# Seven block products in place of eight in sixteen projection chunks of a two-layer fp32 encoder

## The reference, cut to what matters

```
xn = rms_norm(h, ln_mix[l])
proj = xn @ w_in          # layer 0: 256x1024 @ 1024x2500, layer 1: 256x1024 @ 1024x3072
... attention on the split columns of proj, then y @ w_out, h = h + ...
xn = rms_norm(h, ln_ffn[l]);  h = h + hier_moe(xn, ...)   # top-1 group, top-2 of its 8 experts, 32 experts in all
```

## Time and profile before

| what | value |
|---|---|
| three runs | 1186.55, 1188.04, 1189.02 us |
| the profiled execution, device time | 1187.87 us |
| its span | 1186.1 us |
| mean granted TensorE clock | 0.997 of 2.4 GHz |
| PE busy | 1122.9 us of the span |
| DVE, ACT, POOL busy | 217.2, 245.5, 115.7 us |
| HBM read | 441.49 MB, 373 GB/s over the span |

### The profile page before, as it was taken

The page is one execution under the profiler, slowest core; times in us unless marked ns, Lnnn a source line. Parts: engine busy times, 40 slices in busy tenths (PEclk is TensorE's granted clock), DMA queues, the critical chain, the costliest instruction groups (busy, mean ns, idle before and its releaser), DMA issues.

```text
span 1186.1 us, 14020 instructions
## 1 busy us (share of the span) xinstructions
PE 1122.9 (95%) x5006; PEld 503.1 (42%) x5006; DVE 217.2 (18%) x579; ACT 245.5 (21%) x572; POOL 115.7 (10%) x307
## 2 busy tenths in 40 slices
PE   8999999999999988889999999999999998888896
PEld 6876533333333332323487756333333333323232
DVE  2864431000000000000223234300000000000002
ACT  2144251111111111111112233411121111111111
POOL 0003021000110000000000000210011000000000
PEclk9999999999999999999999999999999999999999
DMA  6985589999999999999997354899999999999994
GB/s 242 333 362 228 201 318 429 429 425 429 427 428 428 429 428 429 427 428 428 422 365 309 107 214 184 336 428 426 428 428 427 428 427 430 428 429 427 427 429 203
DMA packets 48586, 443.28 MB, mean 374 GB/s; under 512 B 9564, under 2 KB 14744, under 8 KB 16792
## 3 DMA queue, kind: packets, MB, share of 16 engines
q1 hardware_dynamic: 47464, 441.34, 89.6%
q10 hardware_dynamic: 1072, 1.26, 0.3%
HBM read 441.49 MB, written 1.09 MB: 373 GB/s over the span
## 4 chain that ended last, share of the span: by engine, by line
PE 65%; DMA 31%; ACT 2%; DVE 1%; issue 1%; ACTq 0%; SPq 0%; POOL 0%; POOLq 0%; DVEq 0%
PE PS L1525 22%; DMA places<-in_moe_w_up 15%; PE PS L1534 12%; DMA places<-in_moe_w_gate 11%; PE PS L1277 9%; PE PS L1541 6%; PE PS L1409 5%; PE PS L1281 4%; DMA places<-in_moe_w_down 3%; PE PS L1289 1%; PE PS L1364 1%; DMA bias<-in_c_rel_bias 1%; PE PS L1393 1%; PE PS L1610 1%; PE PS L1494 1%
## 5 line engine op out<-in xcount | busy, mean ns | idle before, releaser
L1525 PE MATMUL PS<-places,mix 128*64 128x512 f32 x1984 | 442.7, 595 | 46.5 <-DMA places<-in_moe_w_up 30.9
L1525 PEld LDWEIGHTS PS<-places,mix 128*64 128x64 f32 x1984 | 140.9, 137 | 339.9 <-issue 276.0
L1534 PE MATMUL PS<-places,gain_att 128*64 128x512 f32 x960 | 213.8, 596 | 0.8 <-ACT gain_att L793 0.5
L1541 PE MATMUL PS<-mix 128*128 128x512 f32 x256 | 124.8, 608 | 0.0
L758 ACT ACTIVATE mix<-acts 128x512 f32 x120 | 76.3, 636 | 227.1 <-PE PS L1525 214.4
L1534 PEld LDWEIGHTS PS<-places,gain_att 128*64 128x64 f32 x960 | 65.9, 137 | 124.5 <-issue 122.7
L1277 PE MATMUL PS<-acts,places 128*128 128x256 f32 x448 | 103.2, 384 | 0.0
L1173 DVE TENSOR_TENSOR mix<-PS,mix 128x512 f32<-128x512 f32 x28 | 19.4, 692 | 418.0 <-PE PS L1525 418.0
L1277 PEld LDWEIGHTS PS<-acts,places 128*128 128x128 f32 x448 | 83.2, 190 | 14.9 <-issue 3.3
L526 POOL TENSOR_TENSOR sm<-sm 128x1 f32<-128x1 f32 x32 | 6.2, 193 | 692.4 <-PE PS L1616 659.5
L565 POOL TENSOR_SCALAR mix<-drop 128x64 f32<-128x64 f32 x128 | 72.2, 584 | 0.0
(11 more groups left out here) (223 smaller groups left out, 633.6 us busy)
## 6 DMA issues: line engine op xcount, KB each, us to landing
places<-in_moe_w_gate SPq DMA_DIRECT2D x56, 2048.0 KB, 24.9
places<-in_moe_w_down SPq DMA_DIRECT2D x54, 2048.0 KB, 32.4
places<-in_moe_w_up SPq DMA_DIRECT2D x52, 2048.0 KB, 30.2
places<-in_moe_w_gate SPq DMA_DIRECT2D x16, 1024.0 KB, 10.6
places<-in_moe_w_up SPq DMA_DIRECT2D x16, 1024.0 KB, 6.4
places<-in_moe_w_down SPq DMA_DIRECT2D x16, 1024.0 KB, 7.5
places<-in_c_w_in SPq DMA_DIRECT2D x12, 1024.0 KB, 20.4
places<-in_ab_w_in SPq DMA_DIRECT2D x8, 1024.0 KB, 14.2
```

The source lines that it names most:

```text
L1525: last = mm(PS[e * SLOTS:(e + 1) * SLOTS, 2 + part, :], xg[:, k, e * SLOTS:(e + 1) * SLOTS], w[e][:, kk, :], start=(k == 0), stop=(k == NK ...
L1534: last = mm(PS[e * SLOTS:(e + 1) * SLOTS, 6 + b, :], hidT[:, k, e * SLOTS:(e + 1) * SLOTS], w[e][:, 512 * b:512 * b + 512], start=(k == 0) ...
L1541: last = mm(PS[:, Y_BANK[q]], pickT[:, t], ye[:, 512 * b:512 * b + 512], start=first, stop=final)
```

## The change

A chunk's product is a 2x2 block product: the tokens in two halves by two halves of the contraction, the weights in two halves of the contraction by two halves of the 256 columns. Each block product is 4 matmuls of 128x128 held by 128 moving columns, and a plain chunk would need eight of them. With sums and differences of blocks made beforehand, seven are enough (Strassen's scheme, in Winograd's form). The change does this from position 4 on in layer 0 (six chunks) and from position 2 on in layer 1 (ten chunks). The four sums of the tokens are made once per layer by DVE; the four sums of the weights once per chunk by POOL, three of them in place, one in a tile that is free then; the seven products go to bank 6 (four) and bank 7 (three); DVE combines them in two visits in place of the one copy. All these chunks are DVE's now, none ACT's.

```diff
+WINO_FROM = (4, 2)
+def nth(layer, pos):
+    return pos - WINO_FROM[layer] + (len(ORDER[0]) - WINO_FROM[0] if layer else 0)
+def sums_before(layer):
+    return 4 if layer and WINO_FROM[0] < len(ORDER[0]) else 0
+def wino(layer, pos):
+    return pos >= WINO_FROM[layer]
 def events(layer):
...
         for quarter in range(4):
             out.append(("tile", pos, quarter))
+            if quarter == 1 and wino(layer, pos):
+                out.append(("sums", pos, None))
             if quarter == 3:
                 out.append(("copy", pos, None))
...
 def by_dve(layer, pos):
-    return ORDER[layer][pos] in BY_DVE[layer]
+    return wino(layer, pos) or ORDER[layer][pos] in BY_DVE[layer]
...
+        token_sum = acts[:, 0:NT * D].rearrange("p (s k n) -> p s k n", s=4, k=4)
+        partial = [at(5640, P), drop0[:, :]]
...
@@ gpsimd
+            def weight_sums(l):
+                for pos in range(WINO_FROM[l], len(ORDER[l])):
+                    n = nth(l, pos)
+                    b11, b12, b21, b22 = (weights_of(pos, i, j) for i in range(2) for j in range(2))
+                    pool.wait_ge(s_place[l][pos], 16)
+                    pool.tensor_tensor(first_sum(l, pos), two_by_two(b12), two_by_two(b11), ALU.subtract).then_inc(s_tsum, 1)
+                    pool.wait_ge(s_tsum, 4 * n + 1)
+                    pool.tensor_tensor(b12, b22, b12, ALU.subtract).then_inc(s_tsum, 1)
+                    pool.wait_ge(s_raw, 2 * n + 1)
+                    pool.wait_ge(s_tsum, 4 * n + 2)
+                    pool.tensor_tensor(b11, b12, b11, ALU.add).then_inc(s_tsum, 1)
+                    pool.wait_ge(s_raw, 2 * n + 2)
+                    pool.wait_ge(s_tsum, 4 * n + 3)
+                    pool.tensor_tensor(b21, b21, b11, ALU.subtract).then_inc(s_tsum, 1)
...
             for l in range(DEPTH):
+                weight_sums(l)
...
@@ vector
+            def token_sums(l):
+                a11, a12, a21, a22 = (tokens(i, j) for i in range(2) for j in range(2))
+                dve.wait_ge(s_xs, 2 * l + 2)
+                dve.tensor_tensor(token_sum[:, 0], a11, a21, ALU.subtract).then_inc(s_xsum, 1)
+                dve.tensor_tensor(token_sum[:, 2], a21, a22, ALU.add).then_inc(s_xsum, 1)
+                dve.wait_ge(s_xsum, sums_before(l) + 2)
+                dve.tensor_tensor(token_sum[:, 1], token_sum[:, 2], a11, ALU.subtract).then_inc(s_xsum, 1)
+                dve.wait_ge(s_xsum, sums_before(l) + 3)
+                dve.tensor_tensor(token_sum[:, 3], a12, token_sum[:, 1], ALU.subtract).then_inc(s_xsum, 1)
+            def four_read(l, pos):
+                n, c = nth(l, pos), quarters(l, pos)
+                p = PS[:, 6].rearrange("p (m n) -> p m n", n=P)
+                dve.wait_ge(s_four, n + 1)
+                if pos > WINO_FROM[l]:
+                    dve.wait_ge(s_pd[l], copies(l, pos - 1))
+                link(dve.tensor_copy(partial[l], p[:, 0]))
+                link(dve.tensor_tensor(c[:, 0], partial[l].unsqueeze(1).broadcast_to((P, 2, P)), p[:, 1:3], ALU.add))
+                dve.tensor_tensor(partial[l], c[:, 0, 1], p[:, 3], ALU.add).then_inc(s_read, 1)
+            def three_read(l, pos):
+                n, c = nth(l, pos), quarters(l, pos)
+                p = PS[:, 7].rearrange("p (m n) -> p m n", n=P)
+                dve.wait_ge(s_proj[l], pos + 1)
+                dve.wait_ge(s_read, n + 1)
+                link(dve.tensor_tensor(c[:, 0, 1], c[:, 0, 1], p[:, 1], ALU.add))
+                dve.tensor_tensor(c[:, 1], partial[l].unsqueeze(1).broadcast_to((P, 2, P)), p[:, 0:2], ALU.add)
+                dve.tensor_tensor(c[:, 0, 1], c[:, 0, 1], p[:, 2], ALU.add).then_inc(s_pd[l], 1)
             def mixer(l):
                 for what, n, _ in events(l):
-                    if what == "copy" and by_dve(l, n):
+                    if what == "copy" and wino(l, n):
+                        three_read(l, n)
+                    elif what == "copy" and by_dve(l, n):
...
                             lambdas()
+                            token_sums(0)
...
+                    elif what == "sums":
+                        four_read(l, n)
...                                                # layer 1, before its mixer
+                    dve.wait_ge(s_proj[l], 1)
+                    token_sums(l)
                 mixer(l)
@@ tensor
+            def seven_products(l, pos, quarter):
+                n, by_column = nth(l, pos), ORDER[l][pos] not in ((4, 5) if l == 0 else (8, 9, 10, 11))
+                def product(bank, m, a, b):
+                    for k in range(4):
+                        held, moved = (b[:, k], a[:, k]) if by_column else (a[:, k], b[:, k])
+                        last = mm(PS[:, bank, m * P:(m + 1) * P], held, moved, start=(k == 0), stop=(k == 3))
+                    return last
+                if quarter == 0:
+                    pe.wait_ge(s_place[l][pos], 16)
+                    if pos == WINO_FROM[l]:
+                        copied(l, ORDER[l][pos - 2])
+                    else:
+                        pe.wait_ge(s_read, n)
+                    product(6, 0, tokens(0, 0), weights_of(pos, 0, 0)).then_inc(s_raw, 1)
+                    product(6, 1, tokens(0, 1), weights_of(pos, 1, 0)).then_inc(s_raw, 1)
+                elif quarter == 1:
+                    pe.wait_ge(s_xsum, sums_before(l) + 3)
+                    pe.wait_ge(s_tsum, 4 * n + 2)
+                    product(6, 3, token_sum[:, 0], weights_of(pos, 0, 1))
+                    pe.wait_ge(s_tsum, 4 * n + 3)
+                    product(6, 2, token_sum[:, 1], weights_of(pos, 0, 0)).then_inc(s_four, 1)
+                elif quarter == 2:
+                    copied(l, ORDER[l][pos - 1])
+                    # first sum of the weights x token_sum 2: four matmuls into bank 7, part 1
...
+                    pe.wait_ge(s_xsum, sums_before(l) + 4)
+                    product(7, 2, token_sum[:, 3], weights_of(pos, 1, 1))
+                else:
+                    pe.wait_ge(s_tsum, 4 * n + 4)
+                    product(7, 0, tokens(1, 1), weights_of(pos, 1, 0)).then_inc(s_proj[l], 1)
```

More of the change, by code:

```diff
@@ L358, in build @@
         s_proj, s_pa, s_pd = per_layer("projected"), per_layer("proj_act"), per_layer("proj_dve")
+        s_xsum, s_tsum, s_raw = sem("token_sums"), sem("weight_sums"), sem("raw_products")
+        s_four, s_read = sem("four_products"), sem("four_read")
         s_is, s_ir, s_drop = sem("index_scores"), sem("index_relu"), sem("selection")
@@ L393, in proj_dst, with quarters, first_sum, tokens @@
             return qkC[:, 2 * c:2 * c + 2] if c < 8 else vC[:, :, (c - 8) * CW:(c - 7) * CW]
+        def quarters(l, pos):
+            c = ORDER[l][pos]
+            dst = proj_dst(l, c)
+            if c in (4, 5) if l == 0 else c >= 8:
+                return dst.rearrange("p i (j n) -> p i j n", n=P)
+            return dst.rearrange("p j (i n) -> p i j n", n=P)
+        def first_sum(l, pos):
+            if pos + 2 < len(ORDER[l]):
+                return quarters(l, pos + 2)
+            j = pos + 2 - len(ORDER[l])
+            if l:
+                return quarters(l, (2, 4)[j])
+            return (kqi[:, 1:3], bias[:, 13:16:2])[j].rearrange("p j (i n) -> p i j n", n=P)
+        def tokens(i, j):
+            return xT[:, 4 * j:4 * j + 4, i * P:(i + 1) * P]
+        token_sum = acts[:, 0:NT * D].rearrange("p (s k n) -> p s k n", s=4, k=4)
+        partial = [at(5640, P), drop0[:, :]]
+        def weights_of(pos, i, j):
+            return place(pos).rearrange("p (k n) -> p k n", n=CW)[:, 4 * i:4 * i + 4, j * P:(j + 1) * P]
         @block.sync
@@ L526, in carry_waits, with two_by_two @@
                 pool.tensor_tensor(spare[:, site:site + 1], half[:, 0:1], half[:, 0:1], ALU.mult)
+            def two_by_two(a):
+                return a.rearrange("p (a b) n -> p a b n", b=2)
+            def weight_sums(l):
[12 more added lines that the diff above has]
+                    pool.tensor_tensor(b21, b21, b11, ALU.subtract).then_inc(s_tsum, 1)
             pool.wait_ge(s_half, 1)
@@ L1246, in copied @@
                 pe.wait_ge((s_pd if by_dve(l, pos) else s_pa)[l], copies(l, pos))
+            def seven_products(l, pos, quarter):
[21 more added lines that the diff above has]
+                    copied(l, ORDER[l][pos - 1])
+                    t1 = first_sum(l, pos)
+                    for k in range(4):
+                        b = t1[:, k // 2, k % 2]
+                        held, moved = (b, token_sum[:, 2, k]) if by_column else (token_sum[:, 2, k], b)
+                        mm(PS[:, 7, P:2 * P], held, moved, start=(k == 0), stop=(k == 3))
+                    pe.wait_ge(s_xsum, sums_before(l) + 4)
[3 more added lines that the diff above has]
+                    product(7, 0, tokens(1, 1), weights_of(pos, 1, 0)).then_inc(s_proj[l], 1)
             def project_tile(l, pos, quarter):
+                if wino(l, pos):
+                    seven_products(l, pos, quarter)
+                    return
```

(1 more changed line is left out.)

## The result

The kernel after took 1194.26 us (median of four, 1192.35 to 1195.95) against 1187.3 us for the kernel before beside it (four runs, 1186.16 to 1189.02): the ratio is 1.0055 [1.0043, 1.0068]. It is slower by some 7 us. The forecast, 1187.3 us and most likely no change, was wrong, though the measured time lies in its range.

A forecast was written before the change was run, and what follows sets the result against it. PE was taken to bound the projections and DMA bytes the late experts, with mixer time passing through to the kernel. Mixer 0 at +5.05 and mixer 1 at -5.6 net -0.55 us: 1187.3 us, range 1182 to 1195.

The forecast's parts named there:

- DVE's reads: Both mixers: two DVE visits add 2.2 us a chunk; PE waiting for normalized rows booked at 0.3 us per mixer.
- POOL's sums: Each chunk: four 128x512 additions at 1.26 us, 5.3 us in all, hidden from PE by 0.15 us in eight chunks.
- rival 2: "POOL late": POOL's third sum makes PE wait, from 1.41 us an operation; at 2.1 us, 1194.8 us; chance 0.20.
- three signs of being wrong: PE waiting for POOL by more than 1 us, counts above 0.115 us, or the clock staying at 1.00.
- Rival 3: Mixer 0: each logit waits behind a DVE visit, 0.5 us at twelve steps, +5.7: 1193.0 us; chance 0.09.
- The matmuls: Seven-product chunks: 0.110 us a count, 6.16 us a chunk, gain 0.75 each, 12.0 us over sixteen before any wait.
- Loads not hidden: New products: weight load and stream one after the other, x56 12.0 us a chunk, 1281 us; chance 0.03.
- The new wait: Mixer 0, position 5: PE waits 6.45 us for DVE's read of position 4, which stands behind `select(1)`.
- The clock: Around the stop at position 5: a fall to 1.2 GHz, 3.4 us of restart at half speed, costing 1.7 us.
- Mixer 1: Second mixer: -0.5 for positions 2 and 3, -6.0 for 4 to 11, +0.6 and +0.3, giving -5.6 us.
- Token sums: Mixer 0: 2.9 us of DVE work before the key copy delays index scores and selection 0.5 us; mixer 1: nothing.
- That a mixer's time is the kernel's: Mixers and experts: the byte stream moves with the mixer, so a microsecond there is one of the kernel, both ways.

The follow-up runs named there:

- the clock kept up: Kernel after plus 14 idle matmuls of 256 columns before PE's wait at position 5 of layer 0: 1190.83 us, ratio 1.0029.
- other banks: Kernel after with position 5 of layer 0 in PSUM banks 2 and 3 in place of 6 and 7: 1190.78 us, ratio 1.0032.
- token sums moved: Kernel after with layer 0's token sums behind the key copy in DVE's list, not ahead of it: 1192.98 us, ratio 1.0043.

## Why the prediction was wrong, point by point

**Failed: the step "DVE's reads", with "POOL's sums".** I timed DVE's operations by rows in which POOL was idle, kept those durations beside POOL's 64 new sums, and booked "0.3 us of such meetings in each mixer". What the prediction held against a slow meeting doesn't bear on it: of the four sums of 726 ns, three have an idle DVE beside them (from 111.54, 114.36 and 116.91 us), and the one from 103.56 meets only an operation that reads PSUM. I had the idea of shared interfaces, but in rival 2 and with the parties the wrong way round: there it made POOL late. POOL was never late: no wait of PE names it. What it did was to hold up DVE, and DVE holds up PE. Measured, of the 9.7 us that mixer 0 lost at its own end 4.4 are gone when the sums are left out, and what is left, 5.3, is near the forecast's 5.05. Its parts are near too: the stop 6.4 us for 6.45, the low clock 5.35 - 3.57 = 1.8 for 1.7; a little luck is in the rest, since the gain per chunk is smaller than said and the end of the mixer costs 0.2 us (27.5 to 27.7 from the last chunk to the first transpose) where I booked 0.6. None of the three signs of being wrong that the prediction names came up: it watched POOL, the counts and the clock, not the lengths of DVE's instructions.

**Where these 4.4 us show.** Position 5 begins at 57.60 us and not at 56.53 as without the sums; 1.0 of it is the one copy of the selection (1.32 us for 0.29). From there to the end of position 9 it is 55.3 us (to 112.88) and not 52.0 (to 106.70 + 1.80): of these 3.3, 2.8 are the extra waits for rows (3.7 with POOL's sums, 0.9 without) and 0.5 the first x32 of position 5 (5.89 for 5.35), which met a later fall of the clock. The further 0.9 us at the experts' end lie within the scatter of that stretch. The groups of after over both mixers:

```profile
L1000 DVE TENSOR_TENSOR gain_att<-gain_att,sm 128x512 f32<-128x512 f32 x12 | 10.4, 867 | 0.4
L1000 DVE TENSOR_TENSOR gain_att<-gain_att,sm 128x256 f32<-128x256 f32 x12 | 7.5, 627 | 0.4
...
L1005 DVE SCALAR_TENSOR_TENSOR gain_att<-gain_att,sm 128x256 f32<-128x256 f32 x4 | 3.0, 738 | 0.1
```

867 ns stand against 692 in the earlier trace rows. In mixer 1 POOL's sums lengthen such operations too, and it costs nearly nothing there, as the gain shows.

**Rival 3, "DVE's queue", had the right engine and the wrong price.** Its 1193.0 us is near the measured 1194.26, but it wanted 0.5 us at each of twelve steps. PE waits for rows five times, from 0.2 to 1.8 us, and one of 0.9 stands in the kernel before too. The two longest of the new ones, 0.6 us before 91.99 and 1.8 before 106.51, stand right behind the slowed multiply of 90.71 and the slowed pair of 103.80 and 104.95.

**The matmuls: right in kind, 1% short.** Counts are 0.1115 us apart (3.57 / 32) and not 0.110, so a chunk takes 6.25 us and gains 0.66 and not 0.75: 1.4 us less over sixteen. "Loads not hidden" is refuted: it needed 0.1234. PE's rows in mixer 1, positions 2 to 11 with all that lies between, last 84.5 us (614.35 to 697.02 + 1.80), 5.3 less than before where I said 6.2; 0.85 of the difference are the counts.

**The new wait: right.** Said 6.45 us; 7.44 in after and 6.4 in the kernel without POOL's sums. DVE's read starts 0.04 us after the last operation of the selection:

```profile
56.05 0.29 DVE L974 TENSOR_SCALAR bias<-bias 128x256 f32<-128x256 f32 x1
56.38 0.29 DVE L1026 COPY mix<-PS 128x128 f32<-128x128 f32 x1
```

**The clock: right in kind, longer than said.** It fell at 55.1 us, within the stop, and came back at 61.96; windows of 1 us of after:

```profile
55.00:56.00 1.00, 0.00 (x0) 0.00 (x0) 0.93 (x3) 0.00 (x0) 0.00 (x0) 0.57 0.97 410
58.00:59.00 1.00, 1.00 (x6) 1.00 (x6) 0.90 (x3) 0.00 (x0) 0.00 (x0) 0.50 1.10 467
...
61.00:62.00 1.00, 1.00 (x7) 1.00 (x7) 0.70 (x2) 0.23 (x1) 0.57 (x1) 0.52 1.03 434
```

From 57.60 to 61.96 PE works at 0.50 (1.2 GHz): 4.4 us, half of it lost, 2.2 us, where I had 3.4 and 1.7. Against the kernel with the clock kept up it is 5.89 - 3.84 = 2.05.

**POOL's sum: right alone, 1.27 us for 1.26.** Beside DVE it is up to 1.72, mean 1.37 for the third sum; the margin of 0.15 us that I gave it at the start of position 5 held. In after this is no test, since PE ran there at the low clock, but in the kernel with the clock kept up the third sum ends at 58.66 + 1.27 = 59.93 us and PE wants it at about 60.1.

```profile
L590 POOL TENSOR_TENSOR places<-places 128x512 f32<-128x512 f32 x16 | 21.9, 1370 | 73.5 <-PE PS L1362 73.5
L587 POOL TENSOR_TENSOR places<-places 128x512 f32<-128x512 f32 x16 | 20.4, 1278 | 1.3
```

**Mixer 1: right**, -5.6 forecast and -6.1 found, of which 5.0 lie in the mixer itself (129.3 us for 134.3 from the experts' end to the first transpose behind mixer 1). **Token sums: right**, 0.5 us forecast; PE's index scores start at 30.16 us and not at 29.60, and without POOL's sums the selection ends at 55.29 and not 54.71. **That a mixer's time is the kernel's:** right; mixer 0's end moved by 9.7 us and the experts' by 10.5.

**Open.** Against their own kernel before, mixer 1's and mixer 0's changes give -4.7 and +13.4 us alone but +7.0 together, not +8.7. The executions of mixer 0 alone had a mean clock of 0.989 to 0.993, those of after 0.991 to 0.993; whether that is all of the 1.7 us is not shown, nor why the falls differ in length. The 0.8 us that the experts of layer 0 add to mixer 0's loss (456.7 for 456.0) are within their scatter, 454.4 to 457.0.

## What to carry to other kernels

Work given to an idle POOL is not free when DVE is on the path: price every DVE instruction that has two SBUF inputs, and every fast SBUF copy, as if it might first wait out one whole POOL instruction, and price the sequence that the next engine waits for, not the shares of busy time. Freeing PE pays where PE ends the stretch (mixer 1: 0.75 to 0.85 us for each product of 0.89). Where the combination of the parts goes to the engine that is already the one met, it pays only as long as nothing slows that engine: four chunks of mixer 0 gave 1.5 to 2.1 us beside a quiet POOL and cost 2.2 by the profile with POOL's sums. Put a new wait on an engine's list only after reading what stands before its release there: a PSUM bank in place of the wait moves the stop to the next thing behind the same list.

## What the runs showed of the hardware that I had not expected

- POOL and DVE hold each other up, in both directions, until the other's instruction is done: an SBUF copy of 128x256 went from 0.29 to 1.32 us, a multiply of 128x512 from 0.69 to 1.24, a sum of POOL from 1.27 to 1.72. Reductions and operations with one input in PSUM are untouched (686 and 689 ns).
- POOL additions that nobody reads made the kernel before 0.26% slower (1190.23 us); longer instructions of DVE are what its profile shows for it. A scan of 128x256 took 1.45 us there and not 0.69.
- The clock fell to 0.50 (1.2 GHz) 5.0 us after PE's last matmul (50.1 to 55.1 us), in the other kernels with a stop after 2.4 (other banks), 2.8 (no sums of POOL), 2.9 (mixer 0 alone) and 3.4 (token sums moved). It came back at 61.96, 4.4 us after PE had started again, in the others after 3.2 to 6.2; fourteen matmuls put into the stop kept it at 1.00.
- A stream of fp32 matmuls of 128 moving columns, each with its own weights, ran at 0.1115 us a count over 32 of them: the loads stay hidden.
